# Putting the gate columns' high and low parts side by side in one weight tile, with VectorE's and TensorE's order around that step

## The reference

```python
h = rmsnorm(x, norm_mix[layer])
proj = (h @ w_in).astype(jnp.float32)
q, k, v, r, glr = jnp.split(proj, ODD_SPLITS, axis=-1)       # glr: 16 columns
gate_logit = glr @ w_gate2.astype(jnp.float32) + b_gate.astype(jnp.float32)
log_a = (jax.nn.log_sigmoid(gate_logit) / GLA_TAU).reshape(B, T, GLA_HEADS, GLA_DK)
```

## Time and profile before

| | us |
|---|---|
| median of 3 executions | 2439.63 (2439.05 to 2439.84) |
| the profiled execution's own time | 2441.21 |
| its span, first to last instruction | 2439.1 |
| busy: TensorE / VectorE / GpSimd / ScalarE | 2423.2 / 1305.2 / 1211.9 / 796.2 |
| mean granted clock of TensorE | 0.993 |
| step `B_ODD_IN` on TensorE | 1143.08 to 1155.06 |
| k step's first matmul | 1168.82 |

### The profile page before, as it was taken

How to read it: one execution, slowest core, us unless ns; L and a number is a source line. 1 busy time by engine, 2 the same in 40 slices (tenths; PEclk the granted TensorE clock), 3 DMA queues, 4 the chain that set the end, 5 groups by cost and what they waited for, 6 DMA issues and landing times. The chain is left out here.

```text
span 2439.1 us, 42031 instructions
## 1 busy us (share of the span) xinstructions
PE 2423.2 (99%) x16160; PEld 2380.3 (98%) x16160; DVE 1305.2 (54%) x2047; ACT 796.2 (33%) x1254; POOL 1211.9 (50%) x1445
## 2 busy tenths in 40 slices
PE   9999999999999999999999999999999999999998
PEld 9999999999999999999999999999999999999998
DVE  6763354345545545566666665554345545445566
ACT  4711442222222223223444564442222222222234
POOL 2454136465675666675201111146565665666681
PEclk9999999999999999999999999999999999999999
DMA  4123031111111111113111111131111111111112
GB/s 151 35 63 89 26 119 44 53 44 44 52 44 44 52 53 41 47 53 117 47 42 63 47 50 58 34 128 44 44 44 53 53 44 44 53 45 43 53 53 83
DMA packets 41023, 140.04 MB, mean 57 GB/s; under 512 B 6320, under 2 KB 10032, under 8 KB 39696
## 3 DMA queue, kind: packets, MB, share of 16 engines
q1 hardware_dynamic: 32768, 106.78, 13.8%
q10 hardware_dynamic: 8080, 30.78, 3.5%
HBM read 120.42 MB, written 14.88 MB: 55 GB/s over the span
## 5 line engine op out<-in xcount | busy, mean ns | idle before, releaser
L732 PE MATMUL PS<-RB,WH 128*128 128x384 f32 (+1 forms) x4368 | 1087.7, 330 | 0.0
L732 PEld LDWEIGHTS PS<-RB,WH 128*128 128x128 f32 x4368 | 773.5, 189 | 7.5 <-issue 3.6
L732 PE MATMUL PS<-RA,WH 128*128 128x272 f32 (+2 forms) x3520 | 769.0, 309 | 1.3 <-DVE RA L1868 0.7
L732 PE MATMUL PS<-RB,WL 128*128 128x384 f32 (+1 forms) x2232 | 731.6, 328 | 0.0
L638 POOL TENSOR_TENSOR WH<-WR,FEW 128x256 fp32r<-128x256 f32 x420 | 320.1, 792 | 622.3 <-PE PS L732 593.0
L732 PEld LDWEIGHTS PS<-RA,WH 128*128 128x128 f32 x3520 | 586.9, 188 | 5.8 <-DVE RA L1868 1.0
L732 PE MATMUL PS<-RA,WL 128*128 128x272 f32 (+2 forms) x1760 | 540.6, 307 | 0.0
L732 PEld LDWEIGHTS PS<-RB,WL 128*128 128x128 f32 x2232 | 421.4, 189 | 0.0
L642 POOL TENSOR_TENSOR WL<-WR,WH 128x256 fp32r<-128x256 f32 x420 | 372.8, 917 | 0.0
L732 PEld LDWEIGHTS PS<-RA,WL 128*128 128x128 f32 x1760 | 330.7, 188 | 0.0
L1967 DVE TENSOR_TENSOR X<-PS,X 128x544 f32<-128x544 f32 x280 | 202.6, 724 | 205.2 <-PE PS L732 205.1
(11 more groups left out here) (237 smaller groups left out, 2370.8 us busy)
## 6 DMA issues: line engine op xcount, KB each, us to landing
WR<-ws SPq DMA_DIRECT2D x189, 512.0 KB, 3.5
EB<-xT ACTq DMA_DIRECT2D x8, 544.0 KB, 5.9
x_spill<-X ACTq DMA_DIRECT2D x8, 544.0 KB, 3.1
EB<-x_spill ACTq DMA_DIRECT2D x8, 544.0 KB, 6.8
GA<-st_gla ACTq DMA_DIRECT2D x4, 1024.0 KB, 4.8
glas_o<-GA ACTq DMA_DIRECT2D x4, 1024.0 KB, 4.6
yT<-X SPq DMA_DIRECT2D x16, 208.0 KB, 1.9
X<-xT ACTq DMA_DIRECT2D x4, 544.0 KB, 6.0
```

Of the source, the lines that this page charges most:

```text
L732: return nc.tensor.matmul(out, lhsT, rhs, start=start, stop=stop, skip_group_check=True)
```

## The change

1. The host repeats the gate columns (and the rows of `wg2`) every 16 columns, six times in 96, where there were zeros between.
2. For step `B_ODD_IN`, GpSimd's new `beside` makes high and low part as `parts` does, then copies the low part over columns 16 to 31, 48 to 63 and 80 to 95 of each block of `WH`, in three more instructions, and only these release the step. One product with this tile gives high columns and low columns side by side; the gate's second product sums them.
3. `first_step` leaves out the third matmul (`WL`) for this step alone: 24 of 72.
4. VectorE makes tile 7's low part ahead of tile 6's addition of squares.
5. `rms(2)` moves from the end of the gate step to behind group 0 of the q step, `rms_end(2)` from there to behind group 1.

```diff
--- before.py
+++ after.py
@@ -366,7 +366,7 @@
 
         w_loaded = [sem("w_loaded0"), sem("w_loaded1")]
         zero_set = sem("zero_set")
-        w_high, w_split = sem("w_high"), sem("w_split")
+        w_high, w_split, low_made = sem("w_high"), sem("w_split"), sem("low_made")
 
         QW = 4
         QC = 1024 // QW
@@ -643,6 +643,23 @@
                                             WH[:, slot, QC * q:QC * (q + 1)].bitcast(F32), ALU.subtract).then_inc(w_split, 1)
 
 
+            def beside(n, slot):
+
+                pool.wait_ge(w_loaded[slot], 16 * (n // 2) + 16)
+                pool.wait_ge(gemm_done, 6 * n - 6)
+                for q in range(QW):
+                    nc.gpsimd.tensor_tensor(WH[:, slot, QC * q:QC * (q + 1)], WR[:, slot, QC * q:QC * (q + 1)],
+                                            ZERO[:, 0:1].to_broadcast([P, QC]), ALU.add).then_inc(w_high, 1)
+                for q in range(QW):
+                    pool.wait_ge(w_high, QW * n + q + 1)
+                    nc.gpsimd.tensor_tensor(WL[:, slot, QC * q:QC * (q + 1)], WR[:, slot, QC * q:QC * (q + 1)],
+                                            WH[:, slot, QC * q:QC * (q + 1)].bitcast(F32), ALU.subtract).then_inc(low_made, 1)
+                second = lambda w: w[:, slot, :].rearrange("p (k b n) -> p k b n", k=KT, n=32)[:, :, 0:3, 16:32]
+                for b in range(3):
+                    pool.wait_ge(low_made, QW)
+                    nc.gpsimd.tensor_tensor(second(WH)[:, :, b, :], second(WL)[:, :, b, :].bitcast(F32),
+                                            ZERO[:, 0:1].unsqueeze(1).to_broadcast([P, KT, 16]), ALU.add).then_inc(w_split, 2 if b == 2 else 1)
+
             def low_part(n, slot):
 
                 pool.wait_ge(w_high, QW * (n + 1))
@@ -704,8 +721,8 @@
                 for slot in range(2):
                     parts(2 * i + slot, i, slot, False)
             mlp(B_MLP0, 0)
-            for slot in range(2):
-                parts(B_ODD_IN + slot, B_ODD_IN // 2, slot, False)
+            beside(B_ODD_IN, 0)
+            parts(B_ODD_IN + 1, B_ODD_IN // 2, 1, False)
             with pool.Fori(HIGH_BY_ACT[0] // 2, HIGH_BY_ACT[-1] // 2 + 1) as i:
                 for slot in range(2):
                     low_part(2 * i + slot, slot)
@@ -782,8 +799,10 @@
                         wh, wl = WH[:, slot, k * P:(k + 1) * P], WL[:, slot, k * P:(k + 1) * P]
                         hi, lo = src[:, 0, k, s:s + size], src[:, 1, k, s:s + size]
                         mm(out, wh, hi, at == 0, False)
-                        mm(out, wh, lo, False, False)
-                        last = mm(out, wl, hi, False, at == KT - 1)
+                        last = mm(out, wh, lo, False, n == B_ODD_IN and at == KT - 1)
+                        if n != B_ODD_IN:
+
+                            last = mm(out, wl, hi, False, at == KT - 1)
                         if at == KT - 1:
                             last.then_inc(gemm_done, 2)
                 if norm is not None:
@@ -1172,10 +1191,12 @@
                     elif u > 0:
                         group(n, n % 2, g, RB, range(KT), 0)
                         if u == 1 and g == 0:
+                            rms(2)
+                        if u == 1 and g == 1:
                             rms_end(2)
                     elif g == 0:
 
-                        first_step(n, RB, 3, 2, after_two=True)
+                        first_step(n, RB, 3, after_two=True)
                 elif kind == "L":
                     h, g = item[1:]
                     s, size = GROUPS[g]
@@ -2032,8 +2053,8 @@
                 if f is not None:
                     for k in range(4, KT):
                         low(f, k, RB, gain)
-                        if k > 5:
-                            add_square(norm, k, SQ2)
+                    for k in (6, 7):
+                        add_square(norm, k, SQ2)
 
             def end_s16(j):
 
@@ -2667,7 +2688,7 @@
     parts.append(mlp(0))
     w = w_in_odd[0]
     low = np.zeros((D, P), w.dtype)
-    for at in (0, 32, 64):
+    for at in range(0, 96, 16):
         low[:, at:at + 16] = w[:, 3072:3088]
     first = {"q": lambda h: 128 * h, "k": lambda h: 512 + 128 * h, "v": lambda h, e: 1024 + 256 * h + 128 * e,
              "r": lambda t: 2048 + 128 * t}
```

## The result

| | us |
|---|---|
| before, median of 14 executions | 2439.62 |
| changed, median of 14 executions | 2444.51 (2443.1 to 2446.46) |
| ratio | 1.0021, 95% interval 1.0013 to 1.0029 |
| profiled execution, own time / span | 2445.43 / 2443.5 |
| forecast (range) | 2442.3 (2438.0 to 2445.8) |

A forecast was written before the change was run, and what follows sets the result against it. TensorE, busy 99% of the span, was taken as the bound: -4.0 + 0.6 + 0.7 + 1.1 + 4.1 = +2.5, taken as +2.7 us by the k step's start, over the median 2439.63 gives 2442.3 us, range 2438.0 to 2445.8.

The forecast's parts named there:

- The matmuls and the tiles: Gate step: 24 fewer matmuls gain 4.0 us; TensorE waits 0.6 us for tile 6 and 0.7 for tile 7.
- The q step's weights: Ahead of the q step: GpSimd's low weights are done at 1153.6, so TensorE waits 1.1 us.
- The three copies: GpSimd's copies in `beside`: 2.1 us, at most 5.3, finished before TensorE needs them, costing nothing.
- The squares: Gate step's end: VectorE's last addition ends near 1155.8 instead of 1154.9, costing nothing with the ones products later.
- The chain: Group 2's ones product through ScalarE and GpSimd to k step's weights: 8.19 us, no slack; TensorE waits 4.1 us.
- the fall in the new waits: Rival around k group 0: clock drops to 0.50, adding 1.7 or 3.4 us; chance 0.14 for 2.2 us or more.
- 0.50 near 1170: Sign of being wrong: a granted clock at half near 1170, around the k step's start.
- main case: Whole kernel: 2.7 us late with at most a short fall of the clock; chance 0.67.
- the case that it gave 0.14: Around k group 0: clock falls for 2.2 us or more of loss; chance 0.14.
- one long fall that costs 3.4 us: Rival over k group 0: 6.8 us at half clock, total 2445.7; part of the 0.14 case.
- My rival with one short fall: Over k group 0: 3.4 us at half clock costs 1.7, total 2444.0; short falls included in the 0.67 case.
- Nothing gives the 2.7 us back: Behind the k step: TensorE stays the bound to the end, so the 2.7 us loss remains.

The follow-up runs named there:

- early k weights: Changed kernel with ScalarE making the k step's high weights right behind tile 7's square, ahead of the norm: 2438.9 us, ratio 0.9996.
- gate tile only: Changed kernel with VectorE's order and the ones products as before, leaving 48 matmuls instead of 72 and GpSimd's copies: 2441.8 us, ratio 1.0007.
- ones products back: Changed kernel with the ones products back at their old place, gate tile and VectorE's order still changed: 2442.1 us, ratio 1.0011.
- ones products only: Kernel before with the ones products moved two token groups back and nothing else: 2444.9 us, ratio 1.0021.
- VectorE's order only: Kernel before with tile 7's low part ahead of tile 6's sum of squares and nothing else: 2440.8 us, ratio 1.0007.
- VectorE's old order: Changed kernel with ScalarE's early q and k high weights, but tile 6's sum of squares ahead of tile 7's low part: 2439.9 us, ratio 1.0004.

## Why the prediction was right, point by point

- **The matmuls and the tiles.** Forecast waits of 0.6 and 0.7 us for tiles 6 and 7; the rows have 0.31 and 0.49. The two are not counted alike: the forecast goes from start to start, the row from the end of the last matmul as the profile shows it, and one of 320 columns is shown for 0.31 us where the next starts after 0.15. Counted from start to start the waits are 0.5 and 0.6. The first block, and each behind a wait, took 1.1 us where I had 1.00.
- **The q step's weights.** Forecast wait 1.1, measured 1.04 in the row and 1.2 from start to start; start of the step 10.3 us after MLP 0, measured 10.5. GpSimd's pace beside VectorE was the right row to take.
- **The three copies.** 2.1 us, measured 2.16, and nobody waited. The number is right by luck: I took 0.70 each because VectorE would be mostly idle, but it adds squares there (in the kernel before from 1137.69 for 1.28 us). Measured were 0.40, 1.45 and 0.40.
- **The squares.** Last addition at 1155.8, measured 1154.13 + 1.29 = 1155.4. Hidden with the ones products moved; where they were put back, TensorE waited 3.05 us for it.
- **The chain.** 8.19 us from the ones product to the k step, measured 1173.08 - 1164.92 = 8.16; wait 4.1, measured 3.95 in the row and 4.1 from start to start. The run that moved only the ones products put this on ScalarE's order by its size, the run that moved only one ScalarE instruction by its cure.
- **The clock was mis-sized.** I gave the fall in the new waits as a rival, for the 4.1 us gap, and the forecast's sum has it at nothing. There were two falls in the profile. The first, behind the short waits ahead of the q step, put the ones product at 21.8 us where 20.0 was forecast: 0.2 of the 1.8 us were there at the q step's start, 1.6 are the fall. The second, behind the long gap, delayed the first gate product by a further 1.6 (35.8 - 30.0 = 5.8 behind the k step, 4.3 before). 2.7 + 1.8 + 1.6 = 6.1 us at that place, 6.0 by the table. The rest of the mixer took 1.7 us less than in the profile of before (429.7 against 431.4, one fall fewer), MLP 0 ended 0.2 sooner and what follows the mixer took 0.2 more, which makes about the 4.4 us of the span. The medians grew by 4.9.
- **What of this was luck.** The prediction names 0.50 near 1170 as a sign of its being wrong, and it came at 1174.2. Its main case, with 0.67, allows one short fall; two, with 3.4 us of lost clock, belong to the case that it gave 0.14. The range held since its upper end was set by one long fall that costs 3.4 us, and two short ones cost the same. My rival with one short fall, 2444.0, is nearer than the forecast, 2442.3; the range held both. The path itself, ScalarE's chain, was no luck: without the first fall the k step is 30.0 - 25.5 - 1.6 = 2.9 us late, where 2.7 was forecast.
- **What the Trainium skill says of it.** TensorE: Matmul & The Clock Gate, Part 1, of the Trainium skill, cited ahead for this rival, has the array go to 1.2 GHz after an idle window. The trace agrees on the level, 0.50. But the first fall began at 1153.7 behind waits of 0.31, 0.49 and 1.04 us with work between them, and in the run that moved only the ones products the clock fell within the wait; the long gap of the change was not the only place to look for it.
- **"Nothing gives the 2.7 us back"** held: from the gate product to the output projection only the step of 1.6 us differs, and no kernel changes anything there.

## What to carry to other kernels

Where the bound engine has no waits, ask for each producer how far ahead of it it is: here one chain had 0.05 us to spare, and a product of 0.3 us that came 4.2 us later uncovered it. When a product is put off because its input is late, list what its consumers do next in program order, and move that ahead first. A gap of TensorE costs its length and can cost the half clock in and behind it, here 1.6 us for each 3.4 us at 0.50 that fell on work.

## What the runs showed of the hardware

- The clock fell not only behind the gap of 3.95 us (0.50 from 1.1 us after its end). In the change's profile it fell behind waits of 0.31, 0.49 and 1.04 us, and in that of the early k weights it stayed at 1.00 behind 0.32, 0.49 and 1.08. It fell within the waits of 2.22 us (gate tile only), 3.05 us (ones products back) and 3.96 us (ones products only), and stayed at 1.00 behind 0.55 us (VectorE's order only) and 1.75 us (VectorE's old order). With the gaps filled by products of ones no fall was seen there.
- GpSimd's copy of 128 elements in 8 pieces of 16 took 0.40 us, and 1.45 us beside VectorE's addition of squares.
- GpSimd's low weights took 0.70 us from start to start alone and 1.75 beside VectorE's low parts. VectorE's low part took 1.35 us with GpSimd idle (the kernel before, 8.7 to 17.1 us) and 1.70 to 1.83 at this boundary; but seven of them beside GpSimd's high weights, from 347 to 418 us, still took 1.34. The high weights that GpSimd began beside these took about 1.67 us, where alone they take 0.61.
